# Unread matmuls behind the last scaled tile of a two-layer decoder trunk

## The chip, the cores and the metric

The kernel runs on one core of one Trainium2 chip. The metric is the device time of one execution in microseconds. The core has five engines that run side by side and meet only at semaphores: TensorE (PE, the matrix engine; its weight loads are listed apart as PEld), VectorE (DVE), ScalarE (ACT), GpSimd (POOL) and SyncE (SP, which here starts transfers).

## The reference

Two layers, each a half-step SwiGLU feed-forward, a mixer (causal pooling and gated linear attention side by side) and a second half-step feed-forward, each behind a residual and a layer norm. 16 learned tokens stand ahead of the 512 given ones and are dropped at the end.

```python
for l in range(DEPTH):                                    # DEPTH = 2, D_MODEL = 1024, D_FF = 2816
    h = layer_norm(a * h + 0.5 * swiglu(h, ffn1_w_gate[l], ffn1_w_up[l], ffn1_w_down[l]), ln1_g[l], ln1_b[l])
    z = h @ w_in[l]
    ...
    y_pool = pool_mixer(u_pool, w_pool[l], pool_scale[l])
    y_gla = gla_mixer(q, k, v, r, g_lr, w_gate_up[l], b_gate[l], gla_norm_g[l])
    y = jnp.concatenate([y_pool, y_gla], axis=-1) @ w_out[l]
    h = layer_norm(a * h + y, ln2_g[l], ln2_b[l])
    h = layer_norm(a * h + 0.5 * swiglu(h, ffn2_w_gate[l], ffn2_w_up[l], ffn2_w_down[l]), ln3_g[l], ln3_b[l])
return h[:, N_META:]
```

## The kernel before

Activations lie transposed: 8 tiles of 128 channels, each with all 528 tokens (16 learned, 512 given) along the free dimension, so a row of a tile is 528 elements or 2112 bytes. Weights arrive from memory as one stream of pieces of 128 x 1024 elements into 4 slots.

Every large product is made of three matmuls of type float32r, a float32 whose low mantissa bits are rounded away: a value is split into a rounded high part and the rest (`x_hi`, `x_lo`; `w_hi`, `w_lo`), and the product is high by high, high by low and low by high, added up in one bank of PSUM. PSUM is eight banks of 512 float32 columns, in the code four tensors `PS[0]` to `PS[3]` of two banks each. A matmul has a stationary operand, which is loaded first (128 rows by up to 128 columns, a LDWEIGHTS record of PEld), and a moving operand whose columns then stream through (up to 512). In layer 0 and for most of layer 1 a matmul has 264 moving columns, half of the tokens (`HALF`). Where only the 512 given tokens are still needed it has 512 or 256, and its moving operand starts at token 16 (`META`) or 272.

Some small products use plain float32 operands: the layer norm's column sums (L808), the spread of the mean (L813) and of the reciprocal root (L824), the pooling product (L902), and a few unread matmuls that are there already (L832 in the norm, L1151 at the start). One plain float32 matmul stands in the trace as two matmul records.

The work of every engine is written out in order in one block for that engine; nothing is reordered by a scheduler. TensorE's block ends with the loop over the two layers. The last thing that it does for layer 1 is `ln_stats` of the last norm (L808 to L832): sums, then the reciprocal root spread over the partitions. After that VectorE centers and scales the 8 tiles of the output (L1857 to L1880), ScalarE applies gain and bias to each (L1380) and counts it in the semaphore `x_full_done`, and SyncE stores each tile (L524). Each of the five norms before adds 5 to `x_full_done`, the last one adds 8.

Of the kernel before, what the change touches and what calls it, by code (L numbers as in the profile page):

```python
# [19 lines left out]
P = 128  # L20
D = 1024
SEQ = 512
DEPTH = 2
META = 16
T = SEQ + META
HALF = T // 2
KC = D // P
# [31 lines left out]
EARLY = 3  # L59
# [240 lines left out]
def build(nc, x_t, first, stream, params, out_t):  # L300
    ctx = ExitStack()
    with ctx:
        def sb(name, shape, dt=F32, where=ctx):
            return where.enter_context(nc.sbuf_tensor(name, shape, dt))

        def sem(name):
            return ctx.enter_context(nc.semaphore(name))
# [3 lines left out]
        with ExitStack() as s9:  # L311
            w_hi = sb("w_hi", [P, SLOTS, PIECE], F32R, s9)
            w_lo = sb("w_lo", [P, SLOTS, PIECE], F32R, s9)
        spare = sb("spare", [P, 2, SLOTS, PIECE])
        X = sb("X", [P, KC, T])
        x_hi = sb("x_hi", [P, KC, T], F32R)
        with ExitStack() as s7:
            x_lo = sb("x_lo", [P, KC, T], F32R, s7)
        x_raw = sb("x_raw", [P, KC, T])
        par = sb("par", [P, C_ALL])  # L320
        ones_mean = sb("ones_mean", [P, P])
# [10 lines left out]
        ident = sb("ident", [P, P])  # L332
        ident_mask = sb("ident_mask", [P, P], I32)
        level_mask = sb("level_mask", [P, len(LEVELS), CH // 2], I32)
        chunk_mask = sb("chunk_mask", [P, T])
# [36 lines left out]
        with ExitStack() as s3:  # L372
            h_hi = sb("h_hi", [P, 2 * THIRDS, T], F32R, s3)
# [26 lines left out]
        PS = [ctx.enter_context(nc.psum_tensor(f"PS{i}", [P, 2, 512], F32)) for i in range(4)]  # L400
# [56 lines left out]
        S = {n: sem(n) for n in names}  # L457
# [7 lines left out]
        LN_PER = 3  # L465
# [138 lines left out]
        def _(pe):  # L604
# [211 lines left out]
            def ln_stats(LN, span, ps):  # L816

                n_tok, blocks = stat_blocks(span)

                def spread_rstd(p):  # L820

                    for i in range(blocks // 2):
                        c = p * blocks // 2 + i
                        m = nc.tensor.matmul(PS[3][:, p, i * n_tok:(i + 1) * n_tok],  # L824
                                             col_rstd[0:n_tok, c:c + 1].to_broadcast([n_tok, P]), ident[0:n_tok, 0:n_tok],
                                             start=True, stop=True)
                    return m

                def unread(count):

                    for i in range(count):
                        nc.tensor.matmul(PS[2 - ps][:, 0, 0:P], ones_mean[:, :], ident[:, :], start=True, stop=True)  # L832

                pe.wait_ge(S["masks"], 1)
                pe.wait_ge(S["consts_dve"], 1)
                pe.wait_ge(S["s1_first"], 2 * LN + 2)
                columns(ps, 0, sum_x, span, 0)
                pe.wait_ge(S["s2_first"], 2 * LN + 2)
                columns(ps, 1, sum_sq, span, 0)
                spread_mean(span, 0).then_inc(S["mean_first"], 1)  # L840
                pe.wait_ge(S["s1_done"], LN * 7 + 7)
                columns(ps, 0, sum_x, span, 1).then_inc(S["mean_acc"], 1)
                pe.wait_ge(S["s2_done"], LN * 7 + 7)
                columns(ps, 1, sum_sq, span, 1).then_inc(S["msq_acc"], 1)
                pe.wait_ge(S["resid_done"], LN * KC + KC)
                spread_mean(span, 1).then_inc(S["mean_spread"], 1)
                unread(2)
                pe.wait_ge(S["rstd_done"], LN + 1)
                spread_rstd(0).then_inc(S["rstd_first"], 1)
                spread_rstd(1).then_inc(S["rstd_spread"], 1)  # L850
                if LN < DEPTH * LN_PER - 1:
                    unread(4)
# [288 lines left out]
            def layer(l, span):  # L1141
                ffn(l, 0, ALL)
                ln_stats(l * LN_PER, ALL, 0)
                mixer(l, span)
                ln_stats(l * LN_PER + 1, span, 2)
                ffn(l, 1, span)
                ln_stats(l * LN_PER + 2, span, 0)
# [5 lines left out]
            for l in range(DEPTH - 1):  # L1153
                layer(l, ALL)
            layer(DEPTH - 1, OWN)

        @block.scalar
        def _(act):
# [394 lines left out]
        def _(dve):  # L1553
# [68 lines left out]
            def add_down(l, f, i, span):  # L1622

                _, p, q = FAST_ORDER[i]
                ps, i_all = bank_set(i), fast_index(l, f, i)
                dve.wait_ge(S["piece_done"], fast_piece(l, f, i) + 2)
                dve.wait_ge(S["c22_done"], i_all + 1)
                dve.wait_ge(S["c12_done"], i_all + 1)
                if p > 0:
                    dve.wait_ge(S["down_evac"], (2 * l + f) * FAST_DOWNS * KC + p * KC)  # L1630
                for odd, op in enumerate((ALU.add, ALU.subtract)):
                    x, y = halves(X[:, 2 * q + odd, :], halved(span)), pair(ps + odd, halved(span))
                    if p == 0:
                        z = V.scalar_tensor_tensor(out=x, in0=x, scalar=ALPHA, in1=y, op0=ALU.mult, op1=op)
                    else:
                        z = V.tensor_tensor(x, x, y, op)
                    z.then_inc(S["down_evac"], 1)
# [707 lines left out]
```

## Time and profile before

| | us |
|---|---|
| median of 2 runs | 1784.16 (1783.89 to 1784.43) |
| span of the profiled execution | 1782.4 |
| TensorE matmul busy | 1770.1 (99%) |
| TensorE weight loads busy | 1733.0 (97%) |
| VectorE / ScalarE / GpSimd busy | 1434.4 / 1168.0 / 340.0 |

The profile lists one execution, from its first to its last instruction. For that execution the page gives the span alone; the runs' median is 1.76 us above it. A matmul record's duration is its way through the engine and overlaps with that of the next one; how often one can follow another is read from their starts.

### The profile page before, as it was taken

What the parts mean: (1) busy time and instruction counts of PE and PEld (TensorE: products, weight loads), DVE (VectorE), ACT (ScalarE), POOL (GpSimd) and SP (SyncE); (2) the same over time, 40 slices, a digit from 0 to 9 for tenths busy, and PEclk for the clock granted to TensorE, in tenths of its full rate; (3) what the DMA queues carried; (4) which work ended last, traced back from release to release, by engine and by line L of the source; (5) the groups of instructions that cost most, each with busy time, mean ns of one, the idle gap of its engine ahead of it and who ended that gap; (6) DMA issues with size and microseconds to landing.
All of it is one profiled execution on the core that took longest, in us unless ns stands there. A gap on an engine that the chain in (4) does not pass through costs nothing.

```text
span 1782.4 us, 37725 instructions
## 1 busy us (share of the span) xinstructions
PE 1770.1 (99%) x14462; PEld 1733.0 (97%) x14462; DVE 1434.4 (80%) x2577; ACT 1168.0 (66%) x2047; POOL 340.0 (19%) x376
## 2 busy tenths in 40 slices
PE   9999999999999999999999999999999999999997
PEld 9999999999999999999999999999998889999996
DVE  7988888668568988888689888886785689888886
ACT  6767666574357667676576767665743577777764
POOL 2111212311011121111311111113110111111113
PEclk9999999999999999999999999999999999999999
DMA  7675766556565766766556757565665656767662
GB/s 217 141 183 129 177 141 144 150 137 141 115 138 110 170 167 148 169 138 159 145 138 145 176 129 180 134 155 139 141 142 117 147 126 149 185 133 185 133 166 72
DMA packets 112561, 263.54 MB, mean 148 GB/s; under 512 B 10752, under 2 KB 35328, under 8 KB 112384
## 3 DMA queue, kind: packets, MB, share of 16 engines
q1 hardware_dynamic: 66592, 167.86, 32.0%
q0 software_dynamic: 45504, 92.29, 30.8%
q8 instruction: 116, 1.90, 0.4%
q10 hardware_dynamic: 288, 0.98, 0.2%
q14 instruction: 61, 0.50, 0.1%
HBM read 259.00 MB, written 2.10 MB: 146 GB/s over the span
## 4 chain that ended last, share of the span: by engine, by line
PE 99%; DVE 0%; DMA 0%; ACT 0%; issue 0%; ACTq 0%; DVEq 0%
PE PS L680 21%; PE PS L682 21%; PE PS L681 21%; PE PS L655 5%; PE PS L656 4%; PE PS L657 4%; PE PS L609 3%; PE PS L611 3%; PE PS L610 3%; PE PS L619 2%; PE PS L645 2%; PE PS L620 2%; PE PS L987 2%; PE PS L808 1%; PE PS L875 0%; PE PS L902 0%
## 5 line engine op out<-in xcount | busy, mean ns | idle before, releaser
L536 POOL DMA_DIRECT2D w_lo<-in_stream x316 | 269.4, 853 | 1336.8 <-ACT w_lo L1202 1301.9
L1198 ACT ACTIVATE s_hi<-s_sum 128x512 fp32r<-128x512 f32 (+1 forms) x496 | 291.1, 588 | 154.2 <-PE PS L682 145.4
L1701 DVE TENSOR_TENSOR s_lo<-s_sum,s_hi 128x512 fp32r<-128x512 f32 (+1 forms) x496 | 294.4, 633 | 2.9 <-ACT s_hi L1198 2.6
L680 PE MATMUL PS<-v_hi,s_hi 128*128 128x264 f32 (+1 forms) x912 | 258.8, 284 | 0.0
L682 PE MATMUL PS<-v_hi,s_lo 128*128 128x264 f32 (+1 forms) x912 | 258.1, 283 | 0.0
L681 PE MATMUL PS<-v_lo,s_hi 128*128 128x264 f32 (+1 forms) x912 | 258.0, 283 | 0.0
L682 PE MATMUL PS<-x_hi,w_lo 128*128 128x264 f32 (+1 forms) x656 | 185.8, 283 | 0.0
L680 PE MATMUL PS<-x_hi,w_hi 128*128 128x264 f32 (+1 forms) x656 | 185.7, 283 | 0.0
L681 PE MATMUL PS<-x_lo,w_hi 128*128 128x264 f32 (+1 forms) x656 | 185.6, 283 | 0.0
L681 PEld LDWEIGHTS PS<-v_lo,s_hi 128*128 128x128 f32 x912 | 172.2, 189 | 0.0
L680 PEld LDWEIGHTS PS<-v_hi,s_hi 128*128 128x128 f32 x912 | 171.8, 188 | 0.0
L682 PEld LDWEIGHTS PS<-v_hi,s_lo 128*128 128x128 f32 x912 | 171.4, 188 | 0.0
L1208 ACT ACTIVATE w_hi<-raw 128x1024 fp32r<-128x1024 f32 (+2 forms) x152 | 147.1, 968 | 8.0 <-DMA raw<-in_stream 8.0
L1202 ACT ACTIVATE w_lo<-raw 128x512 fp32r<-128x512 f32 (+2 forms) x196 | 143.1, 730 | 0.0
L655 PE MATMUL PS<-x_hi,w_hi 128*128 128x264 f32 (+1 forms) x472 | 140.9, 299 | 0.1
L656 PE MATMUL PS<-x_lo,w_hi 128*128 128x264 f32 (+1 forms) x472 | 139.0, 295 | 0.0
L657 PE MATMUL PS<-x_hi,w_lo 128*128 128x264 f32 (+1 forms) x472 | 138.8, 294 | 0.0
L1263 ACT ACTIVATE PS<-PS 128x264 f32<-128x264 f32 (+1 forms) x124 | 46.3, 373 | 136.4 <-PE PS L682 136.4
L682 PE MATMUL PS<-x_hi,s_lo 128*128 128x264 f32 (+1 forms) x448 | 127.9, 286 | 0.0
L681 PE MATMUL PS<-x_lo,s_hi 128*128 128x264 f32 (+1 forms) x448 | 127.2, 284 | 0.0
L680 PE MATMUL PS<-x_hi,s_hi 128*128 128x264 f32 (+1 forms) x448 | 127.1, 284 | 0.0
L680 PEld LDWEIGHTS PS<-x_hi,w_hi 128*128 128x128 f32 x656 | 123.5, 188 | 0.0
(295 smaller groups left out, 5719.8 us busy)
## 6 DMA issues: line engine op xcount, KB each, us to landing
raw<-in_stream SPq DMA_DIRECT2D x164, 512.0 KB, 4.4
w_lo<-in_stream POOLq DMA_DIRECT2D x160, 256.0 KB, 4.6
spare<-in_stream SPq DMA_DIRECT2D x72, 512.0 KB, 6.8
w_lo<-in_stream POOLq DMA_DIRECT2D x60, 512.0 KB, 7.7
raw<-in_stream SPq DMA_DIRECT2D x48, 384.0 KB, 4.2
spare<-in_stream SPq DMA_DIRECT2D x48, 384.0 KB, 5.3
w_lo<-in_stream POOLq DMA_DIRECT2D x96, 192.0 KB, 4.8
X<-in_x_t SPq DMA_DIRECT2D x8, 264.0 KB, 5.8
```

The source lines that it names most:

```text
L536: pool.dma_start(w_lo[:, slot, to], stream[n // RAWS, n % RAWS, :, part], accum_op=ALU.add).then_inc(lo_added[slot], 16)
L609: nc.tensor.matmul(o, hi, rhs_hi[:, k, tok], start=first, stop=False)
L655: yield nc.tensor.matmul(o, hi, rhs_hi[:, k, tok], start=k == 0, stop=False)
L656: yield nc.tensor.matmul(o, hi, rhs_lo[:, k, tok], start=False, stop=False)
L657: yield nc.tensor.matmul(o, lo, rhs_hi[:, k, tok], start=False, stop=k == n - 1)
L680: nc.tensor.matmul(o, hi[:, w], r_hi, start=start and k == 0, stop=False, skip_group_check=True)
L681: nc.tensor.matmul(o, hi[:, w], r_lo, start=False, stop=False, skip_group_check=True)
L682: m = nc.tensor.matmul(o, lo[:, w], r_hi, start=False, stop=stop and k == last, skip_group_check=True)
L1198: nc.scalar.activation(s_hi[:, j - 1, w], s_sum[:, j - 1, w], ACT.Copy).then_inc(S["s_hi_done"], 1)
L1202: nc.scalar.activation(w_lo[:, n % SLOTS, to], of, ACT.Copy, scale=-1.0).then_inc(S["raw_neg"], 1)
L1208: nc.scalar.activation(w_hi[:, n % SLOTS, to], of, ACT.Copy).then_inc(S["raw_hi"], 1)
L1701: V.tensor_tensor(s_lo[:, j - 1, w], s_sum[:, j - 1, w], s_hi[:, j - 1, w].bitcast(F32), ALU.subtract).then_inc(S["s_lo_done"], 1)
```

## The change

Behind the loop over the layers TensorE's block gets a wait for `x_full_done` and then 1214 matmuls whose results nobody reads. The wait's value is (6 - 1) x 5 + 8 = 33, the count after ScalarE's last output tile. A helper `series` issues 20 float32r matmuls at a time, by default with 128 rows, 128 stationary columns, 264 moving columns, and one bank. 59 series follow each other, 1180 matmuls in all. Their stationary and moving operands lie in buffers that the kernel has filled before (`w_hi`, `w_lo`, `x_hi`, `x_lo`, `h_hi`), read as flat rows from a given element on. Then come 34 matmuls of plain float32: 2 of 128 columns, and 8 each of 128, 256, 264 and 512. Nothing else changes; the kernel's own instructions stand in the same order.

```diff
@@ -1153,6 +1153,57 @@
             for l in range(DEPTH - 1):
                 layer(l, ALL)
             layer(DEPTH - 1, OWN)
+
+            pe.wait_ge(S["x_full_done"], (DEPTH * LN_PER - 1) * (KC - EARLY) + KC)
+            flat = {name: t[:, :, :].rearrange("p k t -> p (k t)")
+                    for name, t in (("wh", w_hi), ("wl", w_lo), ("xh", x_hi), ("xl", x_lo), ("hh", h_hi))}
+
+            def series(weights, moving, n=HALF, cols=P, rows=P, count=20, banks=1, chain=False):
+
+                for i in range(count):
+                    w, at = weights[i % len(weights)]
+                    x, xt = moving[i % len(moving)]
+                    ps, bank = (i % banks) // 2 * 2, i % banks % 2
+                    nc.tensor.matmul(PS[ps][0:cols, bank, 0:n], flat[w][0:rows, at:at + cols], flat[x][0:rows, xt:xt + n],
+                                     start=not chain or i == 0, stop=not chain or i == count - 1)
+
+            W, M = ("wh", 0), ("xh", 0)
+            for n in (64, 128, 192, 256, 264, 320, 384, 448, 512):
+                series([W], [M], n=n)
+            for cols in (32, 64):
+                for n in (264, 512):
+                    series([W], [M], n=n, cols=cols)
+            for rows in (32, 64):
+                series([W], [M], rows=rows)
+            for at in (2, 4, 8, 16, 32, 64, 128, 256, 512, 1024, 2048):
+                series([("wh", at)], [M])
+            for at in (2, 4, 8, 16, 24, 32, 64, 128, 256, 512, 1024, 2048):
+                series([W], [("xh", at)])
+            series([W], [M, ("xl", 0)])
+            series([W, ("wl", 0)], [M])
+            series([W, ("wl", 0)], [M, ("xl", 0)])
+            series([W, W, ("wl", 0)], [M, ("xl", 0), M], chain=True)
+            series([W, W, ("wl", 0)], [M, M, ("xl", 0)], chain=True)
+            series([W], [M], chain=True)
+            series([W], [M], banks=2)
+            series([W], [M], banks=4)
+            series([("xl", 0)], [M])
+            series([("xh", 0)], [M])
+            series([("xh", 264)], [M])
+            series([W], [("hh", META)])
+            series([W], [("wh", 0)])
+            series([("wh", 128 * i) for i in range(20)], [M])
+            series([W], [("xh", 264 * i) for i in range(15)])
+            series([("wh", 128 * i) for i in range(20)], [("xh", 264 * i) for i in range(15)])
+            for at in (0, 8, 16):
+                series([("wh", 128 * i) for i in range(20)], [("xh", at + 272 * i) for i in range(15)])
+            series([("wh", 128 * i) for i in range(20)], [("xh", 256 * i) for i in range(15)], n=256)
+            series([("wh", 128 * i) for i in range(20)], [("xh", 512 * i) for i in range(8)], n=512)
+            for x in ("xh", "hh"):
+                nc.tensor.matmul(PS[0][:, 0, 0:P], ones_mean[:, :], ident[:, :], start=True, stop=True)
+            for n in (128, 256, 264, 512):
+                for i in range(8):
+                    nc.tensor.matmul(PS[0][:, 0, 0:n], ones_mean[:, :], chunk_mask[:, 0:n], start=True, stop=True)
 
         @block.scalar
         def _(act):
```

TensorE's program at its end, where the added instructions begin (moving, then stationary operand; rows x moving columns; x20 is one series):

```order
 L832 MATMUL PS<-ident,ones_mean 128x128 x2
 L824 MATMUL PS<-ident,col_rstd 128x128 x4
+L1167 MATMUL PS<-x_hi,w_hi 128x64 x20
+L1167 MATMUL PS<-x_hi,w_hi 128x128 x20
+L1167 MATMUL PS<-x_hi,w_hi 128x192 x20
+L1167 MATMUL PS<-x_hi,w_hi 128x256 x20
+L1167 MATMUL PS<-x_hi,w_hi 128x264 x20
+L1167 MATMUL PS<-x_hi,w_hi 128x320 x20
+L1167 MATMUL PS<-x_hi,w_hi 128x384 x20
+L1167 MATMUL PS<-x_hi,w_hi 128x448 x20
+L1167 MATMUL PS<-x_hi,w_hi 128x512 x20
```

No row moved; these and the other added ones stand behind the last row that was there.

## Rows read from the trace of the kernel before

**Rows 1.** The page: span, busy time, and the chain that ended last.

```profile
span 1782.4 us, 37725 instructions
...
PE 1770.1 (99%) x14462; PEld 1733.0 (97%) x14462; DVE 1434.4 (80%) x2577; ACT 1168.0 (66%) x2047; POOL 340.0 (19%) x376
...
PE 99%; DVE 0%; DMA 0%; ACT 0%; issue 0%; ACTq 0%; DVEq 0%
```

**Rows 2.** Timeline of the end: start, duration (us), engine, line, operands.

```profile
1771.38 0.97 PEld L824 LDWEIGHTS PS<-ident,col_rstd 128*128 128x128 f32 x8
1771.42 1.11 PE L824 MATMUL PS<-ident,col_rstd 128*128 128x128 f32 x8
...
1774.21 6.11 SPq L524 DMA_DIRECT2D out_t<-X  x8
...
1777.74 2.22 ACT L1380 ACTIVATE X<-X,par 128x512 f32<-128x512 f32 x3 [0.40 <-DVE X L1880]
```

**Rows 3.** Stretches of the end: busy us of each engine, PEclk, DMA.

```profile
1772.50:1777.00 4.50, 0.04 (x1) 0.00 (x0) 4.45 (x9) 3.40 (x5) 4.15 (x4) 1.00 0.43 161
1777.00:1778.00 1.00, 0.00 (x0) 0.00 (x0) 0.98 (x2) 0.60 (x2) 0.00 (x0) 0.76 0.66 250
1778.00:1780.00 2.00, 0.00 (x0) 0.00 (x0) 0.90 (x2) 1.96 (x3) 0.00 (x0) 0.50 0.73 277
1780.00:1782.40 2.40, 0.00 (x0) 0.00 (x0) 0.00 (x0) 0.00 (x0) 0.00 (x0) 0.50 0.63 237
```

**Rows 4.** Timeline, TensorE: float32r of 264 columns, first and 25th of a row.

```profile
300.00 0.28 PE L680 MATMUL PS<-x_hi,w_hi 128*128 128x264 f32 x1
...
302.90 0.28 PE L680 MATMUL PS<-x_hi,s_hi 128*128 128x264 f32 x1
```

**Rows 5.** The same, 512 columns (first and 33rd), then 256 columns (first and 48th).

```profile
1755.02 0.39 PE L609 MATMUL PS<-h_hi,w_hi 128*128 128x512 f32 x1
...
1762.47 0.40 PE L611 MATMUL PS<-h_hi,w_lo 128*128 128x512 f32 x1
1762.70 0.28 PE L609 MATMUL PS<-h_hi,w_hi 128*128 128x256 f32 x1
...
1768.21 0.28 PE L611 MATMUL PS<-h_hi,w_lo 128*128 128x256 f32 x1
```

**Rows 6.** Groups by line: rows*stationary columns, rows x moving columns; busy us, mean ns.

```profile
L680 PE MATMUL PS<-x_hi,w_hi 128*128 128x264 f32 x492 | 139.7, 284 | 0.0
...
L875 PE MATMUL PS<-x_lo,w_rank 128*32 128x264 f32 x32 | 8.4, 284 | 0.0
...
L911 PE MATMUL PS<-rank_split,gate_split 96*128 96x264 f32 x8 | 1.3, 284 | 0.0
```

**Rows 7.** Timeline, TensorE: stationary operand of 8 columns, shifted between matmuls, first and 16th.

```profile
1390.23 0.28 PE L1040 MATMUL PS<-sq_hi,rms_weights 128*8 128x256 f32 x1
...
1391.97 0.28 PE L1040 MATMUL PS<-sq_lo,rms_weights 128*8 128x256 f32 x1
```

**Rows 8.** Timeline, weight loads: four of 128 columns for one moving column each.

```profile
1769.55 0.52 PEld L808 LDWEIGHTS PS<-ones_mean,sum_x 128*128 128x128 f32 x4
```

**Rows 9.** Groups by line: mean of one such load; plain float32 records.

```profile
L808 PEld LDWEIGHTS PS<-ones_mean,sum_x 128*128 128x128 f32 x16 | 2.1, 190 | 0.4 <-DVE sum_x L1832 0.3
...
L832 PE MATMUL PS<-ident,ones_mean 128*128 128x128 f32 x64 | 9.1, 277 | 0.0
...
L902 PE MATMUL PS<-ft,par 128*128 128x264 f32 x32 | 8.4, 385 | 0.0
```

**Rows 10.** Timeline: plain float32 in a row, four records each.

```profile
1338.64 1.05 PE L902 MATMUL PS<-ft,par 128*128 128x264 f32 x4
...
1770.98 0.61 PE L832 MATMUL PS<-ident,ones_mean 128*128 128x128 f32 x4
```

**Rows 11.** Stretches of rows 4 and 5: TensorE busy us, PEclk, DMA share, GB/s.

```profile
300.00:320.00 20.00, 20.00 (x168) 1.00 0.48 106
...
1755.02:1762.47 7.45, 7.45 (x34) 1.00 0.00 0
```

**Rows 12.** Timeline, TensorE: the kernel's start.

```profile
1.13 3.78 PE L1151 MATMUL PS<-ones_mean 128*128 128x128 f32 x16 [1.13 <-DVE ones_mean L2235]
5.14 0.56 PE L619 MATMUL PS<-x_hi,w_hi 128*128 128x264 f32 x1 [0.22 <-DVE w_lo L2250]
5.50 0.42 PE L620 MATMUL PS<-x_hi,w_lo 128*128 128x264 f32 x1
5.71 0.42 PE L619 MATMUL PS<-x_hi,w_hi 128*128 128x264 f32 x1
5.93 0.32 PE L620 MATMUL PS<-x_hi,w_lo 128*128 128x264 f32 x1
6.09 0.28 PE L619 MATMUL PS<-x_hi,w_hi 128*128 128x264 f32 x1
6.22 0.28 PE L620 MATMUL PS<-x_hi,w_lo 128*128 128x264 f32 x1
```

## The prediction

> **What bounds the kernel now.** I read the page first: TensorE's matmuls are busy 99% of the span, and the chain of work that ended last is 99% TensorE [rows 1]. So whatever is put between its matmuls is paid in full, and an engine beside it hardly matters. The change, however, puts nothing between them. It stands behind the last one, so the next view is the timeline of the end. TensorE's last record, the spread of the reciprocal root at L824, starts at 1771.42 and ends at 1772.53 us. VectorE and ScalarE then finish the output; the last three tiles of ScalarE run from 1777.74 for 2.22 us, to 1779.96, and the stores follow at once [rows 2]. In the stretch from 1780 to the end no engine computes; the transfers alone are open [rows 3]. The span ends with them at 1782.4. The reader is to see that TensorE has nothing to do in the last 9.9 us, and that the place for more work on it begins where the added wait opens: 33 counts of ScalarE's output tiles are reached with the last tile of all, at 1779.96. Of the time until 1782.4, 2.4 us are cover for the added matmuls. All the rest of them is on the end of the program, one for one, because no other engine has anything left. The time is therefore a sum of 1214 matmuls, and it depends only on how often one can follow another.
>
> **How often one matmul follows another.** A record's duration overlaps with its neighbours', so I divide stretches by counts of starts.
> - float32r of 264 columns: from 300.00 to 302.90 are 24 steps, 0.1208 us each [rows 4].
> - float32r of 512 columns: 32 steps in 7.45 us, 0.2328. Of 256 columns: 47 steps in 5.51 us, 0.1172 [rows 5]. Between them a column costs (0.2328 - 0.1172) / 256 = 0.45 ns.
> - Fewer stationary columns or rows make nothing shorter: with 32 stationary columns and with 96 rows, matmuls of 264 columns have the same mean of 284 ns as with 128 and 128 [rows 6], and with 8 stationary columns 15 steps of 256 columns take 1.74 us, 0.1160 each [rows 7].
> - A load of 128 stationary columns cannot follow another in less than (0.52 - 0.19) / 3 = 0.110 us [rows 8, 9], with one moving column each. That is the floor for matmuls of few columns, if each loads its operand again, as the equal count of loads and matmuls on the page says [rows 1].
> - Plain float32, 264 columns: (1.05 - 0.385) / 3 = 0.222 us per record, two records per matmul; 128 columns: (0.61 - 0.277) / 3 = 0.111 [rows 9, 10].
> - Nothing else will be running. I take the steps of the body as they are, since those of 512 columns ran without any transfer and those of 264 beside a busy memory, and their price per column hardly differs [rows 11].
>
> **The sum.** All at the full clock:
> - 64, 128 and 192 columns, 60 matmuls: no row has float32r under 256 columns. From below, the load's 0.110 bounds it. From above, I take the step of plain float32, twice the columns in two records: 0.222, 0.222 and, at 0.222 / 264 per column, 0.323. I take the floor, because the float32r rows at 256 columns lie only 0.007 above it: 60 x 0.110 = 6.6 us. The upper end is 15.3.
> - 256, 264, 320, 384, 448 and 512 columns: 0.1172 + 0.1208 + 0.146 + 0.175 + 0.204 + 0.2328 = 0.996, times 20 = 19.9 us.
> - 32 and 64 stationary columns with 264 and 512: 2 x (0.1208 + 0.2328) x 20 = 14.1 us.
> - 44 further series of 264 columns (2 of fewer rows, 11 shifted stationary, 12 shifted moving, 8 of alternating operands, chains and banks, 5 of other buffers, 6 of walking operands): 880 x 0.1208 = 106.3 us. The 8 and the 5 are what the body does all the time, in other order. Shifts have rows at some offsets only: the body's halves start at element 0 and 264, the last stages' at 16 and 272, and the 8 column stationary operand of rows 7 moves by one element at a time; none shows a price. For moving starts at 2 or 4 elements there is no row. A gain is not excluded; a loss could be a second pass, at most 0.121 us per matmul. I take nothing.
> - One series each of 256 and 512 columns: 2.3 + 4.7 = 7.0 us.
> - Plain float32: 10 of 128 columns 2.2, and 8 each of 256, 264 and 512 columns at 0.215, 0.222 and 0.431 per record 3.4 + 3.6 + 6.9: 16.1 us.
>
> That is 170.0 us. The clock comes on top. It was granted in full until 1777 and stood at 0.50 (1.2 GHz) from 1778 on, after TensorE had done nothing since 1772.53 [rows 3]. So the series begin at 1.2 GHz. At the kernel's start, steps of 264 columns were still 0.21 to 0.22 us at 5.50 and 5.71, and 0.13 from 6.09 on, 4.9 us after the first matmul at 1.13 [rows 12]. The same 4.9 us at half speed loses 2.4 us. From below the price is near nothing. From above, the clock stays low until the narrow series are through: 60 x 0.11 = 6.6 us, and 2.4 more if it then takes as long as at the start, 9.0.
>
> Begin at 1779.96, 0.05 for the wait, 170.0, 2.4, and 0.16 until the last record is out (0.385 - 0.222, rows 9): TensorE ends at 1952.6. The span was 1782.4 and the runs' median lies 1.76 above it, which I keep: **1954 us**, 170 or 9.5% above before. The 2.4 us of stores are hidden under the new work, since they take no engine that it needs; were they not, they would be 2.4 us more.
>
> **The rivals.**
> 1. The clock stays at 1.2 GHz through the narrow series, which keep the array streaming for a smaller part of the time than the matmuls at the start did. For it: the idle before, and 64 columns beside a load of 128. Against it: at the start, with steps twice as long, it rose within 4.9 us. Up to 6.6 us more: 1961. Chance 0.12.
> 2. Narrow columns or starts at 2 and 4 elements are slow. Narrow at the upper end adds 8.7 us, the two closest shifts of both operands at double step up to 4 x 20 x 0.121 = 9.7: 1963 to 1972. For it: no row excludes it. Against it: rows 7. Chance 0.10.
> 3. Repeated operands run closer. A float32r column costs 0.45 ns where a plain float32 one costs 0.222 / 528 = 0.42; if the surplus comes from the change of operands between matmuls, a step of 264 columns becomes 0.111 and all series are 11 us shorter: 1943. Against it: in the body's triples a matmul already shares an operand with the one before it in every case but one, and the step is 0.1208 all the same. Chance 0.13.
> 4. A matmul starts as soon as its load is through, whatever its columns, because streams overlap: 1180 x 0.110 = 130 in place of 154 us, 1930. Against it: 0.2328 for 512 columns, in a stretch without a wait [rows 5]. Chance 0.03. The Trainium skill (TensorE: Matmul & The Clock Gate, section "Back-to-back issue gap") speaks for this side: it gives about 81 ns per load and matmul at 128 columns and about 131 ns at 512 in a sustained stream. The trace does not agree, with 232.8 ns at 512 columns of float32r, and by that page the series would be shorter still than in this rival.
> 5. Not slower: the time could be closed by the landing of the stores on SyncE's queue and not by TensorE's last matmul. It decides if what is measured does not wait for an engine whose results nobody takes; then the time stays 1784. Against it: the chain is followed back from the last instruction of any engine, and the span runs to it. Chance 0.01.
> 6. The change does not do what it says: the wait opens early, and TensorE starts in its idle stretch at 1772.5 with the clock still full. Then 7.5 and 2.4 us are saved: 1944. Against it: 33 is reached by the last tile alone. Chance 0.01.
>
> **How the numbers follow.** The forecast has a chance of 0.60 and a spread of about 5 us of its own, from the steps' rounding over some 1200 matmuls. The range goes down to 1944 for most of rival 3 and up to 1966 for rival 1 and part of rival 2; what lies outside is under 2 in 10. Before is 1784, and 2% of it, about what a measurement of this kernel can tell from no change, is 36 us: all cases but rival 5 are slower by more. Faster 0.00, same 0.01, slower 0.99.
>
> **What will show it.** The profile after should show the whole trace up to 1780 unchanged, then TensorE alone until about 1952. The clock should be 0.50 for the first series and full within some 5 us. Series of 264 columns should last about 2.42 us, those of 512 4.66, the narrow ones 2.2; 8 plain float32 matmuls of 512 columns 6.9. Shifted series longer than 2.42 would show rival 2, shorter ones at repeated operands rival 3. The prediction is wrong if steps depend on what follows what, which the body's mixture cannot show.

## The result and the profile after

The changed kernel takes 1961.67 us (median of 2 runs, 1960.78 to 1962.56), 1.0994 times the time before, with a 95% interval of 1.0976 to 1.1012. The forecast was 1954, the range 1944 to 1966. The profiled execution took 1960.78 with a span of 1959.0, so 1.78 us lie around the span; before, the runs' median lay 1.76 us above it.

The page, as in [rows 1]: span, busy times, and the chain that ended last, by engine and by line.

```profile
span 1959.0 us, 40221 instructions
...
PE 1949.0 (99%) x15710; PEld 1899.7 (97%) x15710; DVE 1433.9 (73%) x2577; ACT 1167.5 (60%) x2047; POOL 340.1 (17%) x376
...
PE 99%; DVE 0%; DMA 0%; ACT 0%; issue 0%; ACTq 0%; DVEq 0%
PE PS L680 19%; PE PS L682 19%; PE PS L681 19%; PE PS L1167 8%; PE PS L655 4%; PE PS L656 4%; PE PS L657 4%; PE PS L609 3%; PE PS L611 3%; PE PS L610 3%; PE PS L619 2%; PE PS L645 2%; PE PS L620 2%; PE PS L987 1%; PE PS L1206 1%; PE PS L808 1%
```

There are 1248 more matmul records, 1180 and twice 34. VectorE, ScalarE and GpSimd have the busy times of before. The series (L1167) and the plain float32 matmuls (L1206) have joined the chain with 9% of the span: all of the added work is on the path, as forecast.

The timeline where the wait opens, which answers to [rows 2] (ScalarE's line numbers are 51 higher in the changed file):

```profile
1777.18 2.22 ACT L1431 ACTIVATE X<-X,par 128x512 f32<-128x512 f32 x3 [0.40 <-DVE X L1931]
1779.46 4.77 PEld L1167 LDWEIGHTS PS<-x_hi,w_hi 128*128 128x128 f32 x22 [7.67 <-ACT X L1431]
1779.46 4.74 PE L1167 MATMUL PS<-x_hi,w_hi 128*128 128x64 f32 x21 [7.48 <-ACT X L1431]
```

TensorE has idled 7.48 us for ScalarE's last tile and starts 0.06 us behind its end at 1779.40. The body, that is all the kernel's own work ahead of the wait, ended 0.56 us earlier in this execution than in the one before, so from here on I compare stretches that start with the first series.

Stretches of the added work: length, TensorE's busy time (and records; one that a border cuts counts on both sides), PEclk (the granted clock as a share of 2.4 GHz), DMA share, GB/s. They are the series of 64 and of 192 columns, the series of 256 up to the rise of the clock and after it, that of 32 rows, that of 64 rows up to the fall of the clock and after it, the first shifted one up to the rise, the 41 series of 264 columns that follow, and plain float32.

```profile
1779.46:1783.75 4.29, 4.29 (x21) 0.50 0.37 135
...
1788.05:1792.37 4.32, 4.32 (x21) 0.50 0.00 0
1792.37:1794.36 1.99, 1.99 (x11) 0.50 0.00 0
1794.36:1795.68 1.32, 1.32 (x13) 1.00 0.00 0
...
1827.34:1829.94 2.60, 2.60 (x21) 1.00 0.00 0
1829.94:1831.91 1.97, 1.97 (x17) 1.00 0.00 0
1831.91:1833.01 1.10, 1.10 (x6) 0.50 0.00 0
1833.01:1835.32 2.31, 2.31 (x11) 0.50 0.00 0
1836.56:1935.57 99.01, 99.01 (x823) 1.00 0.00 1
1942.53:1958.80 16.27, 16.27 (x69) 1.00 0.00 0
```

The reader is to see two things. Where the clock is full the sum holds almost to the digit: 41 series at the forecast 2.416 us make 99.06, measured 99.01; plain float32 was put at 16.1 and its last drain at 0.16, measured 16.27. And the clock was low twice: from the first matmul until 1794.36, 14.9 us and not 4.9, and once more for 3.4 us from 1831.91, with TensorE busy all the time.

The difference to the forecast, from the first series on (179.59 us, forecast 172.6):

| stretch | forecast | measured | difference |
|---|---|---|---|
| 64 to 192 and the first 256 columns, clock included (1779.46 to 1795.68) | 11.3 | 16.22 | +4.9 |
| 32 rows, 64 rows, first shift (1827.34 to 1836.56) | 7.25 | 9.22 | +2.0 |
| all the rest | 154.0 | 154.15 | +0.1 |

Less 0.55 us for the earlier end of the body, that is the 6.4 us by which the execution ended later than forecast.

### The profile page after: what moved, and what is told of

The parts are those of the page before. It is cut to its first block, busy times and chain, and to the rows that moved or that the text cites. A ratio compares the mean times of both kernels' runs of the same rounds, so it can differ in the third digit from the quotient of the medians.

```text
span 1959.0 us, 40221 instructions
## 1 busy us (share of the span) xinstructions
PE 1949.0 (99%) x15710; PEld 1899.7 (97%) x15710; DVE 1433.9 (73%) x2577; ACT 1167.5 (60%) x2047; POOL 340.1 (17%) x376
## 4 chain that ended last, share of the span: by engine, by line
PE 99%; DVE 0%; DMA 0%; ACT 0%; issue 0%; ACTq 0%; DVEq 0%
PE PS L680 19%; PE PS L682 19%; PE PS L681 19%; PE PS L1167 8%; PE PS L655 4%; PE PS L656 4%; PE PS L657 4%; PE PS L609 3%; PE PS L611 3%; PE PS L610 3%; PE PS L619 2%; PE PS L645 2%; PE PS L620 2%; PE PS L987 1%; PE PS L1206 1%; PE PS L808 1%
## 5 line engine op out<-in xcount | busy, mean ns | idle before, releaser
L1167 PE MATMUL PS<-x_hi,w_hi 128*128 128x264 f32 (+14 forms) x1031 | 150.9, 305 | 7.5 <-ACT X L1431 7.5
L1167 PEld LDWEIGHTS PS<-x_hi,w_hi 128*128 128x128 f32 (+4 forms) x1031 | 140.7, 194 | 14.8 <-ACT X L1431 7.7
```

The lines of the kernel that those rows point to most:

```text
L1167: nc.tensor.matmul(PS[ps][0:cols, bank, 0:n], flat[w][0:rows, at:at + cols], flat[x][0:rows, xt:xt + n], start=not chain or i == 0, stop=n ...
```

## The experiments

Two theories stood against each other. Theory 1: the clock answers to what the matmuls use of the array, columns streamed and rows active, and TensorE's records being back to back is not enough for it. Theory 2: after an idle stretch it stays low for some 15 us, whatever runs. Each run has its own execution of the body, whose end varies by up to 3.8 us, so stretches are taken from the first series on, and places in a run are given from there or in its own time. The runs with 60 matmuls of 192, 128 and 64 columns and with single row counts took 1963.09, 1969.11, 1958.75 and 1982.46 us, one run each; their work is not that of the change, so only their stretches are read.

**The narrow series last.** The loop over column counts is split.

```diff
-            for n in (64, 128, 192, 256, 264, 320, 384, 448, 512):
+            for n in (256, 264, 320, 384, 448, 512):
                 series([W], [M], n=n)
 ...
+            for n in (64, 128, 192):
+                series([W], [M], n=n)
             for x in ("xh", "hh"):
```

> The three series of 64, 128 and 192 moving columns stand behind the other float32r series instead of ahead of them. Theory 1, the clock rises only under matmuls that stream many columns: the 256-column series now meets the low clock, it is full some 5 us after TensorE's start (about 1784.5), 2.4 us are lost there instead of 7.3, and the span is about 1954 us (1959.0 with the change) if the clock stays full through the narrow series, each of 20 x 0.111 = 2.2 us; if the narrow series lower it, up to 6.6 us more. Theory 2, the clock stays low for about 15 us after an idle stretch, whatever runs: it rises at about 1794 again, 7.4 us are lost, span 1959.

Measured: median 1957.53 us (4 runs, 1955.25 to 1959.29), ratio to before 1.0970 [1.0952, 1.0988]; the intervals of this run and of the change overlap, so the times alone decide nothing. The stretches of its profile do: series of 256 up to the rise, all up to the narrow series, the narrow ones up to the fall, the low stretch, the rest.

```profile
1780.24:1783.30 3.06, 3.06 (x14) 0.50 0.51 185
1783.30:1929.38 146.08, 146.08 (x1109) 1.00 0.00 1
1929.38:1933.49 4.11, 4.11 (x39) 1.00 0.01 4
1933.49:1940.31 6.82, 6.82 (x34) 0.50 0.00 0
1940.31:1955.85 15.54, 15.29 (x61) 1.00 0.00 0
```

With broad matmuls (256 columns and more) at the front the clock is full 3.06 us after the first of them, not 15: theory 2 falls. At the back the narrow series take a full clock down, 4.11 us after the first of them and during the series of 128, without a pause of TensorE. From the first series to the end it is 175.61 us, 4.0 less than with the change.

**No idle stretch ahead of the series.** Plain float32 matmuls run in the wait.

```diff
+            for i in range(30):
+                nc.tensor.matmul(PS[2][:, 0, 0:P], ones_mean[:, :], ident[:, :], start=True, stop=True)
             pe.wait_ge(S["x_full_done"], (DEPTH * LN_PER - 1) * (KC - EARLY) + KC)
```

> 30 plain float32 matmuls of 128 columns (6.7 us) are put ahead of the wait, so that TensorE is idle for about 1 us instead of 7.5 us before the first series; the rest is as in the change. Both theories: the clock is still full when the 64-column series begins. Theory 1: it falls again while the three narrow series run (2.2 us each at full clock), so that part of the gain is lost, span between 1952 and 1958 us. Theory 2: it stays full to the end of the narrow ones, whose steps are 0.110 to 0.112 us, span about 1952 us.

Measured: 1959.14 us (4 runs, 1958.9 to 1959.9), span 1957.6. The stretches are the fill, the first series up to the fall, then up to the first matmul of 256 columns, and from there to the rise.

```profile
1772.60:1780.24 7.64, 6.86 (x62) 1.00 0.54 203
1780.24:1784.15 3.91, 3.90 (x35) 1.00 0.39 145
1784.15:1789.63 5.48, 5.48 (x27) 0.50 0.00 0
1789.63:1790.98 1.35, 1.35 (x8) 0.50 0.06 12
```

The narrow series begin at full clock and lose it after 3.91 us; 1.35 us of broad ones bring it back. So the idle stretch is not the cause of the long low one. Filling it saves little, because the narrow series make a low stretch of their own. The steps of 64 columns at full clock: 19 records in the same stretch follow each other at 0.111 to 0.112 us, the forecast's floor of 0.110.

**All rows.** The two series of fewer rows get 128.

```diff
-            for rows in (32, 64):
+            for rows in (P, P):
                 series([W], [M], rows=rows)
```

> The two series of 32 and 64 rows have 128 rows. Theory 1 with few active rows counting like few columns: the second fall of the clock, at 1831.9 with the change, does not appear, the steps of 0.1 us more at the changes of row count disappear too, span about 1957 us. Rival, the fall comes from the series of 32 and 64 stationary columns before them, or of itself: it appears at about the same place, and the span stays above 1958.

Measured: 1961.66 us (one run), span 1959.9, but the body ended 3.8 us later than in the change's execution, which that expectation did not allow for. From the first series on it is 176.66 us, 2.9 less than with the change: 0.8 at the front (the clock rises 13.1 us after the first matmul, 0.2 behind the first of 256 columns), 2.0 in the three series in question:

```profile
1783.24:1796.15 12.91, 12.91 (x61) 0.50 0.13 44
...
1830.21:1837.47 7.26, 7.26 (x62) 1.00 0.00 0
```

7.26 us at full clock where the change took 9.22, and 7.25 was forecast. This one trace does not settle what makes the second fall: it stays out in other traces that still have the series of 32 and 64 rows (told under "The second fall" below), and the series of 32 and 64 stationary columns stand before them here as well. The run with row counts below shows it.

**One series alone.**

Of the added matmuls 20 are left.

```diff
-            for n in (64, 128, 192, 256, 264, 320, 384, 448, 512):
-                series([W], [M], n=n)
+            series([W], [M])
 ...
-            for x in ("xh", "hh"):
 ...
```

> Behind the wait there is one series of 20 matmuls of 264 columns alone. As forecast, the 2.4 us of stores lie beside it: at the low clock it lasts 20 x 0.22 = 4.4 us from 1779.5, TensorE ends at about 1784.1 and the span is about 1784.3 (1782.4 before). Rival, the work starts only behind the stores or lengthens them: span about 1787. Rival, the time does not wait for TensorE: span 1782.4.

Measured: 1787.03 us (one run) beside 1784.23 for the kernel before, span 1785.3. The timeline of its end (start, duration):

```profile
1778.29 2.22 ACT L1396 ACTIVATE X<-X,par 128x512 f32<-128x512 f32 x3 [0.40 <-DVE X L1896]
...
1779.13 1.74 SPq L524 DMA_DIRECT2D out_t<-X  x3
1780.56 4.27 PEld L1167 LDWEIGHTS PS<-x_hi,w_hi 128*128 128x128 f32 x20 [7.68 <-ACT X L1396]
1780.56 4.48 PE L1167 MATMUL PS<-x_hi,w_hi 128*128 128x264 f32 x20 [7.49 <-ACT X L1396]
```

The span ends 0.25 us behind TensorE's last record, at 1785.04, and the series started 0.05 us after ScalarE's last tile (1780.51), beside the stores. The body ended 1.1 us later than in the change's execution, which is the miss against 1784.3. The stores are hidden under the new work, and the time does wait for TensorE: rival 5 falls.

**60 matmuls of 192 columns, at the front and at the back.**

```diff
+            series([W], [M], n=192, count=60)
-            for n in (64, 128, 192, 256, 264, 320, 384, 448, 512):
+            for n in (256, 264, 320, 384, 448, 512):
                 series([W], [M], n=n)
 ...
+            series([W], [M], n=192, count=60)
             for x in ("xh", "hh"):
```

> The first 60 matmuls have 192 moving columns, in place of 20 each of 64, 128 and 192; another 60 of 192 stand behind the other float32r series, where the clock is full. 192 of 256 cycles of a load are columns then. Theory 1a, 192 columns are still too few: at the start the clock stays low for all 12.8 us (steps of 0.213 us) and rises in the series of 256; at the back it falls some 4 us after the first step of 0.112. Theory 1b, 64 and 128 columns alone held it down: it rises some 3 to 7 us after the first matmul, and at the back it stays full, 60 steps of 0.112 us, 6.7 us.

The stretches: front up to the rise, rest of the front, back.

```profile
1781.55:1785.95 4.40, 4.40 (x21) 0.50 0.36 132
1785.95:1790.41 4.46, 4.46 (x41) 1.00 0.00 0
1938.13:1944.81 6.68, 6.68 (x61) 1.00 0.00 0
```

Theory 1b: 192 columns raise the clock, 4.40 us after the first of them, and keep it full for 6.68 us.

**60 matmuls of 128 columns instead.** The same edit with `n=128`.

> As the run with 60 matmuls of 192 columns at the front and 60 at the back, with 128 columns in their place. 192 let the clock rise and kept it full. Theory 1c, a matmul of 128 columns, half of its load's time, is still enough: the clock rises some 3 to 7 us after the first matmul, and at the back 60 steps of 0.112 us stay at full clock, 6.7 us; only 64 columns held it down in the change. Theory 1d, 128 columns are too few: at the front it stays low for all 12.8 us (60 x 0.213) and rises in the series of 256; at the back it falls some 4 us after the first step.

The stretches: front, the series of 256 up to the rise, back.

```profile
1780.46:1793.32 12.86, 12.86 (x61) 0.50 0.12 45
1793.32:1796.79 3.47, 3.47 (x17) 0.50 0.00 0
1944.16:1950.81 6.65, 6.65 (x62) 1.00 0.00 0
```

Neither 1c nor 1d, but half of each: 128 columns do not raise a low clock in 12.86 us, and they do not lower a full one in 6.65.

**60 matmuls of 64 columns at the back.** The front starts with 256 columns; `series([W], [M], n=64, count=60)` stands ahead of the plain float32 matmuls, and the series of 128 and 192 are gone.

> The front begins with the series of 256; 60 matmuls of 64 columns stand behind the other float32r series, where the clock is full, and there are none of 128 and 192. 128 columns did not raise the clock at the front and did not lower it at the back. Theory 1e, 64 columns are what lowers it: it falls some 3 to 5 us after the first of them, and the rest of the 60 take 0.213 us. At the front it rises some 3 to 7 us after the first matmul of 256. Rival, no count of columns lowers a full clock while loads follow each other without a gap (the falls of the earlier runs came from the mixture): 60 steps of 0.112, 6.7 us, at full clock.

The stretches: the series of 256 up to the rise; 64 columns up to the fall, the rest of them.

```profile
1780.91:1785.02 4.11, 4.11 (x19) 0.50 0.39 141
1930.51:1935.21 4.70, 4.70 (x44) 1.00 0.02 3
1935.21:1938.88 3.67, 3.67 (x19) 0.50 0.00 0
```

64 columns alone lower a full clock, 4.70 us after the first of them. At the front 256 columns needed 4.11 us here, 3.47 in the run before and 3.06 with the narrow series last; the 4.40 us of 192 columns are therefore no sign that fewer columns raise it later.

**Row counts one at a time.** 60 matmuls each of 32, 64 and 96 rows, with series of 128 rows between.

```diff
-            for rows in (32, 64):
-                series([W], [M], rows=rows)
+            series([W], [M], rows=32, count=60)
             for at in (2, 4, 8, 16, 32, 64, 128, 256, 512, 1024, 2048):
                 series([("wh", at)], [M])
+            series([W], [M], rows=64, count=60)
 ...
+            series([W], [M], rows=96, count=60)
             series([W], [M, ("xl", 0)])
```

> 60 matmuls each (7.2 us at full clock) of 32, of 64 and of 96 active rows, with full-row series between them; 264 columns throughout. Theory 1 with active rows counted: with 32 rows the clock falls some 4 us after the first of them and rises again a few us after full rows are back; with 64 the same or nothing, with 96 nothing. Rival, a fall needs the change of the row count itself (three changes within 5 us, as in the change): no fall here, since each count stands for 7 us.

The stretches: 32 rows up to the fall, the rest of them, 128 rows up to the rise; 64 rows; 96 rows.

```profile
1828.81:1833.15 4.34, 4.34 (x37) 1.00 0.00 0
1833.15:1838.73 5.58, 5.58 (x27) 0.50 0.00 0
1838.73:1843.39 4.66, 4.66 (x22) 0.50 0.00 0
1867.58:1875.06 7.48, 7.48 (x62) 1.00 0.00 0
1904.25:1911.45 7.20, 7.20 (x63) 1.00 0.01 2
```

32 rows alone lower the clock after 4.34 us, without another change of row count; 64 and 96 do not in 7 us. 64 rows bring pauses at the changes of row count too (7.48 us for 60, where 7.20 is 0.120 each) and keep the clock, so such pauses alone are not the cause. In the change the fall came among the matmuls of 64 rows, 4.57 us after the first of 32.

**The same work in another order.** The fill ahead of the wait, and nothing narrow or of few rows next to its like.

```diff
+            for i in range(30):
+                nc.tensor.matmul(PS[2][:, 0, 0:P], ones_mean[:, :], ident[:, :], start=True, stop=True)
             pe.wait_ge(S["x_full_done"], (DEPTH * LN_PER - 1) * (KC - EARLY) + KC)
 ...
-            for n in (64, 128, 192, 256, 264, 320, 384, 448, 512):
+            for n in (256, 264, 64, 320, 384, 128, 448, 512, 192):
                 series([W], [M], n=n)
 ...
-            for rows in (32, 64):
-                series([W], [M], rows=rows)
+            series([W], [M], rows=32)
             for at in (2, 4, 8, 16, 32, 64, 128, 256, 512, 1024, 2048):
                 series([("wh", at)], [M])
+            series([W], [M], rows=64)
```

> The same series in another order, with the 30 plain matmuls ahead of the wait: each narrow series (64, 128, 192 columns) stands behind two or more broad ones, and the series of 32 and of 64 rows are apart. Theory 1: no narrow stretch is longer than 2.6 us, the clock is never low, and from the first series to the end of the span are the forecast 170.0 us, 0.2 for the last drain, 0.3 for the end and 0.4 at the changes of row count: 170.9, 8.7 less than with the change; the median about 1953. If the forecast's steps were wrong too, the stretch differs from 170.9 with a full clock. Rival, a narrow series lowers the clock for a few us wherever it stands: up to 3 us lost at each, 176 or more.

Measured: 1952.57 us (4 runs, 1951.69 to 1953.46), ratio to before 1.0940 [1.0922, 1.0959], whose interval lies below that of the change. Its stretches: the series of 64, 128 and 192 columns, that of 32 rows, and all of the added work; then the line on its core with the mean granted clock.

```profile
1785.50:1787.65 2.15, 2.15 (x22) 1.00 0.00 0
1794.16:1796.34 2.18, 2.18 (x22) 1.00 0.00 0
1805.01:1807.21 2.20, 2.20 (x21) 1.00 0.00 0
1821.33:1823.93 2.60, 2.60 (x22) 1.00 0.00 0
1780.60:1951.72 171.12, 170.88 (x1248) 1.00 0.01 4
```

```profile
core 0: 1951.7 us, clock 1.000
```

The clock is never low, and the work takes 171.12 us where 170.9 was expected. The same series with 30 more matmuls take 9.1 us less (1961.67 to 1952.57), where the 30 matmuls alone had taken off 2.5 (1959.14). No version of this kind can beat the kernel before, since the work is unread.

## Why the prediction was right, and where it was not

**Place and cover: right.** TensorE starts with ScalarE's last tile, the stores lie beside it, and the span ends 0.25 us behind its last record; the run with one series shows it with the cover alone.

**Steps at full clock: right.** The forecast put them at 170.0 us; the run in another order gives 171.12, of which 0.25 is the end, 0.16 the last drain and some 0.4 the changes of row count. The narrow series take 2.15 to 2.20 us each at the floor of the weight load, as forecast, so float32r of under 256 columns is not slow at full clock: that half of rival 2 falls, and with it the upper end of 15.3. Neither shift, nor bank, nor order of operands costs more than 0.07 us in a series of 20. Single widths are off by up to 0.1 us a series, both ways (256 columns 2.40 for 2.34, 512 columns 4.58 for 4.66), and cancel.

**The clock at the front: the term that was mis-sized.** The prediction put the low clock at the 4.9 us of the kernel's start and the loss at 2.4. It was low for 14.9 us and cost 7.3 (16.22 us, where these four series take 8.93 at full clock in the other order and in the 256 columns' own steady steps of 0.120). Rival 1 had the mechanism, with a chance of 0.12 that was too low, and the range reaches to the measured time because its upper end was set for that rival and part of rival 2. That its 1961 is also the measured time is luck in part: of its 6.6 us the front took 4.9, and the second fall, which it did not have, brought 2.0. The start's matmuls were plain float32, two records of 128 columns each; the first series are single records of 64 [rows 12]. I took the time that the clock needed there for a property of the clock. The runs show that it depends on what runs: 3.06 to 4.11 us with 256 columns, 4.40 with 192, not within 12.86 with 128. In the change it rose 1.99 us into the series of 256, in the run with all rows 0.2 us into it; which of the series of 192 and 256 raised it there is not separated.

Nor was the 4.9 us more than one reading. The kernel's start is the same in all runs, and in the other traces the steps of its matmuls shorten at other times: in the run with 192 columns after 3.1 us, within the first 16 records, in the run with row counts only at 7.03, after 5.9.

```profile
1.13 3.49 PE L1151 MATMUL PS<-ones_mean 128*128 128x128 f32 x16 [1.13 <-DVE ones_mean L2288]
```

```profile
6.80 0.39 PE L620 MATMUL PS<-x_hi,w_lo 128*128 128x264 f32 x1
7.03 0.28 PE L619 MATMUL PS<-x_hi,w_hi 128*128 128x264 f32 x1
```

What sets the time between these bounds was not tried.

**The second fall: missing.** No step had a clock that falls under matmuls back to back. As far as the run with row counts shows, the 32 rows did it, for 2.0 us with the changes of row count. It does not come every time: with the same 20 matmuls of 32 rows it came in the change, in the run with the fill and, just behind the 64 rows, in that with 128 columns, and not in four others (in the run with the narrow series last, PEclk is 1.00 through that whole stretch). What decides between them is open. The changed kernel's other run was 1.8 us longer, of the size of such differences.

**The other rivals.** Repeated operands do not run closer (rival 3): series with one operand pair over and over take 2.40 to 2.47 us, with alternating operands exactly 2.40. Streams do not overlap so that the load alone counts (rival 4): the first series of 512 columns takes 4.58 us per 20, 0.229 each. The Trainium skill (TensorE: Matmul & The Clock Gate, section "Back-to-back issue gap"), with about 131 ns at 512 columns, does not agree with that. The same page of the Trainium skill says in "What's actually happening" that a monitor grants the clock by how busy TensorE has been of late. The trace agrees only if busy is not read as in the profile: TensorE's records and its loads are 100% busy in the 12.9 us at half clock.

## What to carry to other kernels

A TensorE that is busy without a gap can still run at 1.2 GHz: look at PEclk beside the busy share wherever float32r matmuls have 128 moving columns or fewer, or use 32 rows (plain float32 of 128 columns, two records each, kept the clock full in the fill, 7.64 us at 1.00). Put narrow matmuls between broad ones, or few in a row, and put broad ones first after an idle stretch; 30 unread matmuls ahead of a wait save little if what follows is narrow. When a clock's delay is taken from another place of the trace, compare how many columns and rows the matmuls there use before taking its length, and look at more than one trace.

## What was not expected of the hardware

- The clock did not rise and fall with the same matmuls. In these runs, each read from one trace, 64 moving columns lowered it in 4.70 us, 128 neither lowered nor raised it, 192 raised it in 4.40 us. With 264 columns, 32 active rows lowered it in 4.34 us, 64 and 96 kept it.
- float32r settles into steady steps. The rows are the series of 320 and 384 columns, then six series of alternating or chained operands, and the last series of 256.

```profile
1798.11:1801.03 2.92, 2.92 (x22) 1.00 0.00 0
1801.03:1804.50 3.47, 3.47 (x22) 1.00 0.02 5
```

```profile
1889.77:1904.17 14.40, 14.40 (x122) 1.00 0.01 1
1935.57:1937.96 2.39, 2.39 (x22) 1.00 0.03 7
```

  That is 0.146, 0.1735 and 0.120 us a step, and 0.120 for 256 columns as for 264. At one column per cycle of 2.4 GHz 256 columns would be 0.107 us, 264 would be 0.110 and 512 would be 0.213 (an estimate; plain float32 of 264 columns, taken as two cycles per column, would be 0.220 us per record and takes 0.222 [rows 10]). So a float32r matmul takes 0.010 to 0.016 us more at these widths, and 0.020 at 448 (4.13 us for 20). The surplus is not quite the same everywhere: in the body 256 columns follow each other at 0.1172 us [rows 5], and shifted operands here take up to 0.124 for 264. Why float32r pays it was not tried.
- Going to 32 or 64 active rows and back costs about 0.1 us each way: 2.60 us for 20 matmuls of 32 rows at full clock, where 20 of 128 rows take 2.42. 96 rows have none of it: 60 matmuls take 7.20 us, 0.120 each.
